# Two gate banks and two score banks in the windowed attention, and the low parts of the merged rows made one by one

## What is computed

```python
# first block
x = x + (g_a * y_attn + g_b * y_conv) @ w_out[l]

# second block, layer 1: windowed attention with a sink, 16 heads, 4 kv heads
sc = jnp.einsum('bnqkgd,bnskd->bnkgqs', qb, kb).astype(jnp.float32) * scale + bias
m = jnp.maximum(jnp.max(sc, axis=-1, keepdims=True), sink_l)
p = jnp.exp(sc - m)
denom = jnp.sum(p, axis=-1, keepdims=True) + jnp.exp(sink_l - m)
o = jnp.einsum('bnkgqs,bnskd->bnqkgd', (p / denom).astype(v.dtype), vb)
return (oc * jax.nn.silu(gc)) @ w_out
```

## Time and profile before

| | |
|---|---|
| median of 3 runs | 1543.19 us (1537.08 to 1543.99) |
| the profiled execution's own time | 1543.9 us |
| its span, first to last instruction | 1541.5 us |
| mean granted TensorE clock | 0.952 of full speed |
| busy: PE, PE weight load, DVE, ACT, POOL | 92%, 72%, 54%, 26%, 43% |
| merging with `y` units, then `wout` | from 379 us, and from 423 us |
| windowed attention, 32 steps | from 1350.8 to 1476.7 us |

### The profile page before, as it was taken

How to read it: one execution, slowest core, us unless ns; L and a number is a source line. 1 busy time by engine, 2 the same in 40 slices (tenths; PEclk the granted TensorE clock), 3 DMA queues, 4 the chain that set the end, 5 groups by cost and what they waited for, 6 DMA issues and landing times. The chain is left out here.

```text
span 1541.5 us, 19578 instructions
## 1 busy us (share of the span) xinstructions
PE 1425.6 (92%) x7318; PEld 1116.8 (72%) x7318; DVE 839.7 (54%) x1411; ACT 403.3 (26%) x891; POOL 660.1 (43%) x523
## 2 busy tenths in 40 slices
PE   5989879999999999997999799899999889989897
PEld 5879656778778888885787778666566777866676
DVE  4995657834443689999681353333455223045632
ACT  2000235623111211122110221144445202144520
POOL 4671522235655667776496326410000153631220
PEclk9996989999999999998999889999999999999998
DMA  5420200112343245554552312100000122311011
GB/s 195 149 83 27 70 15 28 42 42 82 96 150 110 96 150 192 191 191 150 205 179 81 116 55 82 55 28 14 14 1 1 42 68 74 96 42 41 29 42 55
DMA packets 37377, 130.24 MB, mean 84 GB/s; under 512 B 4400, under 2 KB 4656, under 8 KB 37040
## 3 DMA queue, kind: packets, MB, share of 16 engines
q1 hardware_dynamic: 27072, 94.16, 19.0%
q10 hardware_dynamic: 10224, 34.94, 6.5%
HBM read 126.98 MB, written 2.10 MB: 84 GB/s over the span
## 5 line engine op out<-in xcount | busy, mean ns | idle before, releaser
L934 POOL TENSOR_TENSOR wlo<-raw,whi 128x1024 fp32r<-128x1024 f32 x171 | 420.4, 2458 | 14.3
L930 POOL TENSOR_TENSOR whi<-raw,ones 128x2 fp32r<-128x2 f32 x171 | 53.2, 311 | 826.0 <-DMA raw<-in_w 826.0
L427 PE MATMUL bank<-ysplit,whi 128*128 128x512 f32 x960 | 298.7, 392 | 3.7 <-DVE ysplit L1901 3.7
L427 PE MATMUL bank<-hhi,whi 128*128 128x512 f32 x648 | 273.2, 422 | 20.8 <-DVE arena L1876 7.8
L427 PE MATMUL bank<-hlo,whi 128*128 128x512 f32 x648 | 259.5, 400 | 0.0
L427 PE MATMUL bank<-hhi,wlo 128*128 128x512 f32 x648 | 259.1, 400 | 0.0
L427 PEld LDWEIGHTS bank<-ysplit,whi 128*128 128x128 f32 x960 | 180.0, 189 | 40.7 <-issue 4.1
L931 POOL TENSOR_SCALAR whi<-raw 128x1022 fp32r<-128x1022 f32 x171 | 192.3, 1125 | 0.0
L427 PE MATMUL bank<-ysplit,wlo 128*128 128x512 f32 x480 | 187.5, 391 | 0.0
L427 PEld LDWEIGHTS bank<-hhi,whi 128*128 128x128 f32 x648 | 125.7, 194 | 60.0 <-issue 23.6
L427 PEld LDWEIGHTS bank<-hhi,wlo 128*128 128x128 f32 x648 | 125.7, 194 | 28.1
(11 more groups left out here) (251 smaller groups left out, 2021.2 us busy)
## 6 DMA issues: line engine op xcount, KB each, us to landing
raw<-in_w SPq DMA_DIRECT2D x171, 512.0 KB, 3.5
arena<-in_ada ACTq DMA_DIRECT2D x48, 512.0 KB, 4.3
xbuf<-in_xT SPq DMA_DIRECT2D x8, 256.0 KB, 4.5
first<-in_w ACTq DMA_DIRECT2D x1, 2048.0 KB, 8.1
xbuf<-in_w ACTq DMA_DIRECT2D x1, 2048.0 KB, 7.9
xbuf<-in_xT ACTq DMA_DIRECT2D x8, 256.0 KB, 3.1
out_t<-xbuf SPq DMA_DIRECT2D x8, 256.0 KB, 2.2
first<-in_uq ACTq DMA_DIRECT2D x1, 768.0 KB, 6.8
```

What stands on the lines that cost most here:

```text
L427: m = mm(b[:, :], w[:, s, k * P:(k + 1) * P], x, start=(k == 0 and part == 0), stop=(k == DC - 1 and part == 2))
L930: g.tensor_tensor(whi[:, s, 0:2], raw[:, s, 0:2], ones[:, :], ALU.mult)
L934: g.tensor_tensor(wlo[:, s, :], raw[:, s, :], whi[:, s, :].bitcast(F32), ALU.subtract)\
```

## The change

The first block's attention gets a pool of its own for its gate units, with the one bank that it had. In the second block's attention bank 3 goes from the scores to the gate units: scores use banks 1 and 2, gate units banks 0 and 3 in turn. In the first block, the low part of chunk `i - 1` is made right behind the addition of chunk `i`; that of chunk 7 behind the loop.

```diff
-C_FILL, C_S, C_T, C_O, C_R = (0,), (1, 2, 3), (4, 5), (6,), (7,)
-N_S, N_O = (1, 2), (3, 6)
+N_FILL, N_S, N_O = (0,), (1, 2), (3, 6)
+C_FILL, C_S, C_T, C_O, C_R = (0, 3), (1, 2), (4, 5), (6,), (7,)
...
-                    part = unit(*(("ga", i // TT) if i < n else ("gb", 0)), inline=False, pool=C_FILL)
+                    part = unit(*(("ga", i // TT) if i < n else ("gb", 0)), inline=False, pool=N_FILL)
...
+            def merged_low(i):
+                dve.wait_ge(*act_did.at(("mhi", i)))
+                V.scalar_tensor_tensor(hlo[:, i, :], merged[:, i, :], 0.5, hhi[:, i, :].bitcast(F32),
+                                       ALU.mult, ALU.subtract).then_inc(*dve_did.up(("m", i)))
+
...
                 V.tensor_tensor(merged[:, i, :], merged[:, i, :], ytmp, ALU.add)\
                     .then_inc(*dve_did.up(("mg", i)))
-            for i in range(DC):
-                dve.wait_ge(*act_did.at(("mhi", i)))
-                V.scalar_tensor_tensor(hlo[:, i, :], merged[:, i, :], 0.5, hhi[:, i, :].bitcast(F32),
-                                       ALU.mult, ALU.subtract).then_inc(*dve_did.up(("m", i)))
+                if i:
+                    merged_low(i - 1)
+            merged_low(DC - 1)
```

## The result

The changed kernel takes 1522.78 us (median of six runs, 1518.21 to 1526.01) against 1539.56 for the kernel before in the same session: a ratio of 0.9888, 95% interval [0.986, 0.9915], so 13 to 22 us faster. The profiled execution took 1524.71 us by its own time, with a span of 1522.3; before it was 1543.9 and 1541.5.

A forecast was written before the change was run, and what follows sets the result against it. The prediction took PE, busy 92% of the span, and its waits to bound the kernel. From the profiled 1543.9 us, 6.0 for merged rows and 8.6 for gate units gave 1529.3; it forecast 1529.0, range 1523 to 1536.

The forecast's parts named there:

- Merged rows, -6.0: Last y unit to wout 0: PE's waits for low parts and the half clock behind them go, saving 6.0 us.
- The worry about POOL: Rival in the merged rows: a POOL split stretches low part 6 or 7, costing 1.3 us (1530.3); chance 0.04.
- Gates, -8.6: Windowed attention: gate units find a free bank, 1.05 us in each of five pairs and 3.33 at p = 1.
- Two score banks, 0: Windowed attention: scores wait for the second half of c_max, put at zero cost, with bounds 0 and 2.5 us.
- the one foreseen at p = 1: Attention at p = 1: step 4's scores need both halves of c_max 3 and start 0.31 us later.
- The 0.3 and 0.5 us margins: Second step of an attention pair: 0.3 us to spare for the scores, 0.5 us for the values.
- Sum: Whole kernel: 1543.9 of the profiled execution less 6.0 and 8.6 gives 1529.3; forecast 1529.0 us.
- The range's low end: Whole kernel: 1523 us, reached if half-clock stretches in stages left alone come out shorter; chance 0.05.
- The wait changed its name: Rival at each pair's second step: PE waits for c_max instead of gates, 2.5 us in all (1531.5); chance 0.15.
- The clock at p = 1: Rival in the attention: the half-clock stretch at p = 1 stays, costing 1.6 us (1530.6); chance 0.04.
- Both parts did what they say: Against the rival that only the merged rows (1537.2) or only the gates (1534.6) gain; chance 0.09.
- The slower case, scores as the chain: Rival in the attention: c_max holds scores in all 31 steps, about 0.65 us each, 20 us (1557); chance 0.03.

The follow-up runs named there:

- after_again: The changed kernel run once more with no edit; 1525.01 us, ratio 0.989 to the kernel before.
- gate_from_3: Changed kernel with the second block's gate banks taken in the order 3, 0 instead of 0, 3; 1525.87 us, ratio 0.991 to the kernel before.
- before_again: The kernel before run again against itself with no edit; 1537.13 us, ratio 0.9987.
- compress_later: Changed kernel with the first block's 128 narrow compression matmuls moved behind token unit 1; 1508.09 us, ratio 0.979 to the kernel before.
- out_first: Changed kernel with gate banks in the order 3, 0 and c_out written ahead of the next pair's gates on DVE; 1520.81 us, ratio 0.9868 to the kernel before.

## Why the prediction's parts were right and its time was not

*Merged rows, -6.0.* Right, to 0.1 us in the trace (11.47 to 5.44), 5.4 in the runs. Low parts 6 and 7 were made between 426.5 and 428.0 and wanted at 427.96 and 428.64: margins of 0.8 and 0.65 us, where the prediction had 1.0 and 0.9. The last addition (L1710) took 1.07 us where the old one had taken 0.94, and all behind it came later by that. Both began inside a split of POOL's (L934) and ended some 0.55 us behind its end, so where the split falls sets how long they take. The worry about POOL was about the right thing, though it had the low parts hit and the addition ahead of them was. The next split began at 427.72, and `x` came in time.

One group of rows was misread: "seven near 0.68 and one of 2.88 us". The three figures of rows 5 don't say that. Taken singly in the trace, six low parts took 0.68 us, one 1.52 (from 427.69, beside L931) and one 2.88 (from 429.14, beside L934). No term hangs on it.

*Gates, -8.6.* Right in its parts. Five pairs lost 1.00 to 1.04 each (15.65 to 15.69 became 14.65), forecast 1.05. p = 1 took 2.73, forecast 2.74, with a wait of 0.28 for `c_max` where 0.31 was forecast; `og` 1 waits 0.74 as before. One part of the term is missing, put at nothing without a word: the half clock at the last pair (11.80 us before, 10.25 after). The five profiles with one gate bank have 11.7 to 11.8 us there; of those with two and DVE's old order, three have 10.25, after_again 11.23 and gate_from_3 11.45. So with a second gate bank the clock gives back 0.4 to 1.5 us more, and the traces of the changed kernel show 9.0 and 10.0 for the term. Why the clock holds there better after the shorter pairs was not tried.

*Two score banks, 0.* Right to within 0.43 us of waits, 0.28 of them the one foreseen at p = 1. The 0.3 and 0.5 us margins at the pair's second step held.

*Sum.* This is **the step that failed**: "1543.9 - 6.0 - 8.6 = 1529.3 from the profiled execution; its own time lies 0.7 above the median of the runs". The terms were taken from one execution, the slowest of three (and by that sentence's own 0.7 the forecast would be 1528.6). In its next 23 runs the kernel before has a median of 1540.67, and 1540.8 and 1540.9 in the sessions after that: 3.2 lower. From there the same terms give 1526.1, and the changed kernel measured 1522.8 and 1525.0 in two sessions. What is left, 1 to 3 us, is no larger than the intervals.

The two profiles say what the base had in it. From 1543.9 to 1524.71 is 19.2 us, 4.6 more than the terms. Of these 3.4 are the wait of L663, which the base had at 10.9 us and the changed kernel at 7.5, and 1.5 are the clock at the last pair; what remains is -0.3. The sum costs both at nothing. Neither is at L566: both profiles ran it at half clock.

*The range's low end* failed with it. The text saw that "others, in stages that the change leaves alone (slices 4 and 5 of rows 1 are at 6 to 8 tenths), may come out shorter or longer", and gave 0.05 to the time getting as low as 1523. (The digits are slices 4 and 6; slice 5 is at 9.) Slice 4 holds the narrow matmuls. With nearly all of them at half clock in the profiled execution, a swing there could hardly go up and could go down by 9 us, as before_again showed. A range that took the base from the median and the swing from that slice would have reached to about 1517, and the changed kernel's quickest runs are at 1517.3 and 1518.2.

*The rivals.* The wait changed its name for 0.4 us, not 2.5. POOL took margin, not time. The clock at p = 1 was at 1.00. Both parts did what they say. The slower case, scores as the chain, shows in nothing.

## What to carry to other kernels

A forecast made of differences needs the level of many runs as its base, not of one profiled execution: look in that profile for long waits and for stretches at half clock that can only get better, and let the range lean that way. Here a second bank for a step that is released once per round took away the whole wait, while a third bank for one that is released every step was worth 0.4 us at most: read each margin before moving a bank. And a wait ahead of a long run of narrow matmuls can cost several times its length (here 4.0 us cost 18.7), so place such a run where its operands are long ready.

## What the hardware showed beyond that

**27.5 us of narrow matmuls, all at half clock.** PE was at full clock when it came to stand for 4.0 us, and the clock fell in that wait. Then it ran 62-column matmuls back to back for 27.5 us with no idle time in the trace, all of it at half clock, and the clock came back only in the wide matmuls of the next unit. The changed kernel by windows (busy by engine, then granted clock):

```profile
100.00:107.00 7.00, 6.94 (x31) 5.43 (x29) 6.90 (x5) 0.62 (x2) 5.79 (x5) 1.00 0.23 75
107.00:110.97 3.97, 0.00 (x0) 0.03 (x1) 3.91 (x3) 0.58 (x1) 3.28 (x4) 0.78 0.40 132
110.97:138.50 27.53, 27.53 (x129) 27.53 (x130) 20.15 (x25) 0.00 (x0) 3.75 (x2) 0.50 0.00 1
138.50:144.00 5.50, 5.50 (x16) 4.31 (x16) 2.42 (x6) 0.00 (x0) 0.00 (x0) 0.56 0.00 0
144.00:150.00 6.00, 6.00 (x30) 4.96 (x29) 2.06 (x9) 1.28 (x3) 0.00 (x0) 1.00 0.28 87
```

The same matmuls behind wide ones, without a wait, kept the full clock to their end in the profiles of all three kernels that have them later; `compress_later` by windows:

```profile
113.60:128.10 14.50, 14.50 (x132) 14.50 (x131) 14.40 (x16) 0.95 (x2) 6.93 (x4) 1.00 0.12 37
```

Behind waits of 1.1 and 1.4 us (before_again, above) the first half still ran at full clock and the second mostly did not. In out_first PE had the wait of 1.1 us alone, and the clock fell between 111 and 112 us, some 2 us behind the first of the narrow matmuls, and the rest ran at half. Whether a shorter wait does no harm was not tried.

**One VectorE instruction, 1.22 or 3.41 us.** Ahead of the feed-forward net's first down matmul DVE has no idle time, and PE waits for it. L1737 (L1733 in the kernel before) multiplies two tiles that lie in SBUF and sums them up. There the timelines of DVE and POOL in the changed kernel show:

```profile
698.46 1.22 DVE L1737 CUSTOM_DVE_ANT_0 arena<-arena 128x1024 f32<-128x1024 f32 x1
...
711.30 3.41 DVE L1737 CUSTOM_DVE_ANT_0 arena<-arena 128x1024 f32<-128x1024 f32 x1
```

```profile
710.93 2.70 POOL L934 TENSOR_TENSOR wlo<-raw,whi 128x1024 fp32r<-128x1024 f32 x1
```

The long one starts inside a split of POOL's and lasts 1.1 us beyond that split's end; the short one takes 1.22, and POOL's L931 that came 0.1 us behind its start, at 698.56, took 2.03 where the next two took 1.05. The twelve profiles bear it out. All 222 of these instructions that began with POOL idle took 1.21 to 1.23 us. All 216 that began inside an L934 took 1.27 to 3.42 us and ended 1.08 or 1.09 us behind its end. The last additions of the merging, which read two tiles in SBUF as well, do the same: each of the 96 began inside an L934 and ended 0.54 to 0.56 us behind it.

The Trainium skill, SBUF — State Buffer, section "SBUF: two separate sides", has a rule for this: a VectorE instruction with two inputs in SBUF and a GpSimd instruction that reads SBUF exclude each other on the shared ports, and whichever starts first keeps them to its end. The trace agrees, by the numbers above.

This is also what moves the wait of L663. In all twelve profiles DVE works without idle time for 49.7 to 54.5 us ahead of it, through the same 55 instructions, and PE's wait is that time less 43.5 us, 6.2 to 11.1. Between the first two profiles the 3.4 us of difference lie in instructions with two inputs in SBUF alone, some longer and some shorter by how the splits fell. No run took the splits away, and why they fall as they do in one execution is open.
